# Seven block products in place of eight for half of a SwiGLU input matrix, on one TensorE

## The reference

```python
x = x + 0.5 * swiglu_ffn(rmsnorm(x, ffn1_norm), ffn1_w_in, ffn1_w_out)
proj = rmsnorm(x, mix_norm) @ w_in           # q, k, v of 16 heads, and 8 forget columns
... two kinds of attention, 8 heads each ...
x = x + mixed @ w_out
x = x + 0.5 * swiglu_ffn(rmsnorm(x, ffn2_norm), ffn2_w_in, ffn2_w_out)

def swiglu_ffn(x, w_in, w_out):
    gate, up = jnp.split(x @ w_in, 2, axis=-1)      # w_in is 2048 x 11008
    return (jax.nn.silu(gate) * up) @ w_out          # w_out is 5504 x 2048
```

## Time and profile before

| | |
|---|---|
| median of 3 runs | 1899.95 us (1899.06 to 1902.18) |
| profiled execution | 1897.12 us, its span 1895.3 us |
| mean granted clock of TensorE | 0.995 |
| instructions | 20376 |
| moved by DMA | 347.13 MB, mean 183 GB/s |

### The profile page before, as it was taken

The page is one execution under the profiler, slowest core; times in us unless marked ns, Lnnn a source line. Parts: engine busy times, 40 slices in busy tenths (PEclk is TensorE's granted clock), DMA queues, the critical chain, the costliest instruction groups (busy, mean ns, idle before and its releaser), DMA issues.

```text
span 1895.3 us, 20376 instructions
## 1 busy us (share of the span) xinstructions
PE 1858.9 (98%) x8470; PEld 1545.2 (82%) x8470; DVE 946.6 (50%) x1051; ACT 818.2 (43%) x971; POOL 26.9 (1%) x37
## 2 busy tenths in 40 slices
PE   6999999999999999999999999999999999999999
PEld 5888888888988888877777788888888888988887
DVE  4444444454544554365555555545444444444443
ACT  5444444444434444344444445444444444433332
POOL 1000000000000000000000000000000000000000
PEclk9999999999999999899999999999999999999999
DMA  6655555555655557344454455555655555556553
GB/s 225 213 197 181 197 185 192 190 187 172 206 194 186 181 200 241 108 137 156 145 166 155 164 170 177 180 198 179 198 180 199 182 195 180 192 185 210 202 202 116
DMA packets 175643, 347.13 MB, mean 183 GB/s; under 512 B 5808, under 2 KB 14064, under 8 KB 175424
## 3 DMA queue, kind: packets, MB, share of 16 engines
q1 hardware_dynamic: 172304, 337.92, 54.1%
q10 hardware_dynamic: 2080, 3.94, 0.6%
q0 software_dynamic: 1168, 3.97, 0.5%
HBM read 343.70 MB, written 3.68 MB: 183 GB/s over the span
## 4 chain that ended last, share of the span: by engine, by line
PE 93%; DVE 3%; ACT 2%; issue 1%; DMA 1%; ACTq 0%; DVEq 0%
PE acc L248 30%; PE acc L250 30%; PE acc L249 29%; ACT whi L458 2%; DVE wlo L676 1%; PE aux L275 1%; DMA x<-x 1%; PE aux L265 1%; PE aux L327 0%; DVE act_f L782 0%; PE aux L378 0%; PE aux L370 0%; PE aux L369 0%; PE aux L340 0%; PE aux L339 0%
## 5 line engine op out<-in xcount | busy, mean ns | idle before, releaser
L676 DVE TENSOR_TENSOR wlo<-raw,whi 128x1024 fp32r<-128x1024 f32 (+1 forms) x656 | 790.8, 1206 | 913.5 <-ACT whi L458 911.7
L458 ACT ACTIVATE whi<-raw 128x1024 fp32r<-128x1024 f32 (+1 forms) x656 | 684.6, 1044 | 1036.6 <-PE acc L250 1036.6
L248 PE MATMUL acc<-whi,xs 128*128 128x512 f32 (+1 forms) x1792 | 700.1, 391 | 3.7 <-DVE wlo L676 3.6
L250 PE MATMUL acc<-whi,xs 128*128 128x512 f32 (+1 forms) x1792 | 692.3, 386 | 0.0
L249 PE MATMUL acc<-wlo,xs 128*128 128x512 f32 (+1 forms) x1792 | 691.8, 386 | 0.0
L248 PEld LDWEIGHTS acc<-whi,xs 128*128 128x128 f32 x1792 | 337.4, 188 | 68.4 <-issue 5.1
L250 PEld LDWEIGHTS acc<-whi,xs 128*128 128x128 f32 x1792 | 337.3, 188 | 66.3
L249 PEld LDWEIGHTS acc<-wlo,xs 128*128 128x128 f32 x1792 | 337.6, 188 | 63.7
L248 PE MATMUL acc<-whi,act 128*128 128x512 f32 x688 | 268.1, 390 | 0.0
L250 PE MATMUL acc<-whi,act 128*128 128x512 f32 x688 | 267.7, 389 | 0.0
L249 PE MATMUL acc<-wlo,act 128*128 128x512 f32 x688 | 267.7, 389 | 0.0
(11 more groups left out here) (116 smaller groups left out, 519.4 us busy)
## 6 DMA issues: line engine op xcount, KB each, us to landing
raw<-ffn_w_in SPq DMA_DIRECT2D x160, 1024.0 KB, 4.9
raw<-ffn_w_out SPq DMA_DIRECT2D x80, 1024.0 KB, 4.9
raw<-w_in SPq DMA_DIRECT2D x48, 1024.0 KB, 5.0
raw<-w_out SPq DMA_DIRECT2D x16, 1024.0 KB, 4.9
raw<-ffn_w_in SPq DMA_DIRECT2D x16, 768.0 KB, 4.3
raw<-ffn_w_out SPq DMA_DIRECT2D x8, 768.0 KB, 4.3
x<-x ACTq DMA_DIRECT2D x4, 512.0 KB, 13.4
bias_vectors<-bias_vector POOLq DMA_DIRECT2D x1, 1536.0 KB, 9.0
```

The source lines that it names most:

```text
L248: mm(banks[b][:, 0:w], stationary[:, k, 0, tok], hi, start=k == 0, stop=False, skip_group_check=True)
L250: last = mm(banks[b][:, 0:w], stationary[:, k, 1, tok], hi, start=False, stop=k == k_total - 1, skip_group_check=True)
L458: A(whi[:, h % SLOTS, 0:n_el], raw[:, slot, first:first + n_el], ACT.Copy).then_inc(weights_hi, 1)
L676: V.tensor_tensor(wlo[:, h % SLOTS, 0:n_el], raw[:, slot, first:first + n_el], whi[:, h % SLOTS, 0:n_el].bitcast(f32), ALU.subtract).then_ ...
```

## The change

The first unit of each FFN is computed as before (`plain_unit`), with x_turn of part n placed right ahead of the halves that use it in the first FFN. In the other ten, k-tiles 0 to 7 are still plain halves (G0, G1 for the gate, U0, U1 for up: 8 halves of 12 matmuls). K-tiles 8 to 15 are taken as a 2 x 2 by 2 x 2 block product: blocks of tokens by k-tiles 8 to 11 and 12 to 15, and these by gate and up columns. Seven products (T1, B11, T2, B21, T3, B22, T4), each of two halves of 6 matmuls (`form`), take the place of eight. Their x side is a block of `xs` or one of four sums in `sf`, made once per FFN (`form_inputs`, `form_sums`, `form_splits`). Their weight side is a loaded piece, or one of four sums of pieces made on DVE in each unit (`sum_t1` to `sum_t4`, 128 x 2048 each), which are split like pieces. Parts of the results are copied out of PSUM by ACT (three copies a unit) and added by DVE (`w_done`, `gate_added` twice, `c11_done`).

`raw` has 6 slots in the FFNs. A slot is free when its last reader is done, which for B11 and B21 is `sum_t4`. SP issues the 8 pieces of a unit in the order of `LOAD`, and x's four parts stand in SP's queue too, each ahead of a weight piece.

The activation is kept in float32 (`act`), and `ffn_out` makes two passes over its 43 tiles with 1024 columns each, a half being one k-tile by 1024 columns; ACT and DVE split `act` once in each pass, two tiles at a time, into windows of 4 slots (`act_window_hi`, `act_window_lo`). Updates of x come after a pass: parts 0 and 1 in the second pass, parts 2 and 3 after it.

```diff
-RAW_SLOTS, SLOTS = 3, 4
+RAW_SLOTS, QKV_RAW_SLOTS, SLOTS, ACT_SLOTS = 6, 3, 4, 4
+ACT_PAIRS = -(-FT // 2)
...
+T1, B11, G0, T2, B21, T3, G1, B22, T4, U0 = 0, 2, 4, 6, 8, 10, 12, 14, 16, 18
+UNIT_HALVES = 22
+LOAD = {"B11": 0, "B12": 1, "B22": 2, "G0": 3, "B21": 4, "G1": 5, "U0": 6, "U1": 7}
...
+            def free(n):
+                for u in range(2):
+                    if IN_P[u] <= n < OUT_P[u]:
+                        j, i = (n - IN_P[u]) // 8, (n - IN_P[u]) % 8
+                        if j == 0:
+                            return weights_lo, IN[u] + 2 * i + 2
+                        if i in (LOAD["B11"], LOAD["B21"]):
+                            return sums_done, 4 * ((UNITS - 1) * u + j)
+                        last = {LOAD["B12"]: T3, LOAD["B22"]: B22, LOAD["G0"]: G0, LOAD["G1"]: G1, LOAD["U0"]: U0, LOAD["U1"]: U0 + 2}[i]
+                        return weights_lo, unit_half(u, j) + last + 2
+                    end = (QKV_P, END_P)[u]
+                    if OUT_P[u] <= n < end:
+                        c, q = (n - OUT_P[u]) // ACT_PAIRS, (n - OUT_P[u]) % ACT_PAIRS
+                        return weights_lo, OUT[u] + FT * c + min(2 * q + 2, FT)
+                return weights_lo, QKV + 2 * (n - QKV_P) + 2
...
+                    if j == 0:
                         for q in range(4):
-                            piece(n, w_in[:, 4 * q:4 * q + 4, col:col + UNIT_W[j]], 4, UNIT_W[j])
-                            n += 1
-                for c in range(N_OUT):
-                    for t in range(0, FT, 4):
...
+                            if u == 0:
+                                sp.dma_start(x[:, :, q * W:(q + 1) * W], x_rows[:, :, q * W:(q + 1) * W]).then_inc(x_loaded[q], 16)
+                            elif q == 3:
+                                sp.wait_ge(logit_ready, N_HEADS)
+                            piece(n + q, w_in[:, 4 * q:4 * q + 4, gate], 4, w)
+                        for q in range(4):
+                            piece(n + 4 + q, w_in[:, 4 * q:4 * q + 4, up], 4, w)
+                    else:
+                        piece(n + LOAD["B11"], w_in[:, 8:12, up], 4, w)
+                        piece(n + LOAD["B12"], w_in[:, 8:12, gate], 4, w)
+                        piece(n + LOAD["B22"], w_in[:, 12:16, gate], 4, w)
+                        piece(n + LOAD["G0"], w_in[:, 0:4, gate], 4, w)
+                        piece(n + LOAD["B21"], w_in[:, 12:16, up], 4, w)
+                        piece(n + LOAD["G1"], w_in[:, 4:8, gate], 4, w)
+                        piece(n + LOAD["U0"], w_in[:, 0:4, up], 4, w)
+                        piece(n + LOAD["U1"], w_in[:, 4:8, up], 4, w)
...
+            def form(h, bank_out, stationary, w, start):
+                for i in range(2):
+                    pe.wait_ge(weights_lo, h + i + 1)
+                    slot = (h + i) % SLOTS
+                    for k in range(2):
+                        hi, lo = whi[:, slot, k * w:(k + 1) * w], wlo[:, slot, k * w:(k + 1) * w]
+                        st_hi, st_lo = stationary(2 * i + k, 0), stationary(2 * i + k, 1)
+                        mm(bank_out[:, 0:w], st_hi, hi, start=start and i == 0 and k == 0, stop=False, skip_group_check=True)
+                        mm(bank_out[:, 0:w], st_hi, lo, start=False, stop=False, skip_group_check=True)
+                        last = mm(bank_out[:, 0:w], st_lo, hi, start=False, stop=i == 1 and k == 1, skip_group_check=True)
+                    last.then_inc(weights_used, 1)
...
+            def plain_unit(u):
+                Y, V, Z, X = unit_banks(0)
+                base, w, s = IN[u], UNIT_W[0], 2 * u
+                for hh in range(IN_HALVES):
+                    if u == 0 and hh % 2 == 0:
+                        x_turn(0, hh // 2)
+                    pe.wait_ge(x_ready, 16 * s + 2 * hh + 2)
+                    plain(base + hh, 2 * hh, (Z, X), (True, True), w, KT - 1)
+                    if u == 0 and hh == 7:
+                        small_products()
+                    if u == 1 and hh == 2:
+                        x_turn(2, 3)
+                for hh in range(IN_HALVES):
+                    plain(base + IN_HALVES + hh, 2 * hh, (V, Y), (True, True), w, KT - 1)
+            def unit(u, j):
+                Y, V, Z, X = unit_banks(j)
+                base, w, first = unit_half(u, j), UNIT_W[j], (UNITS - 1) * u + j - 1
+                blk0, blk1 = slice(0, P), slice(P, 2 * P)
+                if j == 1:
+                    pe.wait_ge(silu_done, 2 * (UNITS * u + 1))
+                    pe.wait_ge(s_ready, 4 * (u + 1))
+                    if u == 0:
+                        pe.wait_ge(vec_ready, 1)
+                else:
+                    pe.wait_ge(gate_added, 2 * first)
+                form(base + T1, Z, lambda k, t: sf[:, 0, k, t, :], w, True)
+                form(base + B11, Y, lambda k, t: xs[:, 8 + k, t, blk0], w, True)
+                pe.wait_ge(copied, 3 * first + 1)
+                for i in range(2):
+                    plain(base + G0 + i, 2 * i, (Z, X), (False, True), w, -1)
+                pe.wait_ge(copied, 3 * first + 2)
+                form(base + T2, Y, lambda k, t: sf[:, 1, k, t, :], w, False)
+                act_turn(u, j - 1)
+                form(base + B21, V, lambda k, t: xs[:, 12 + k, t, blk0], w, True)
+                pe.wait_ge(copied, 3 * first + 3)
+                form(base + T3, Y, lambda k, t: sf[:, 2, k, t, :], w, False)
+                for i in range(2):
+                    plain(base + G1 + i, 4 + 2 * i, (Z, X), (False, False), w, 7)
+                form(base + B22, Z, lambda k, t: sf[:, 3, k, t, :], w, False)
+                pe.wait_ge(w_done, first + 1)
+                form(base + T4, Y, lambda k, t: xs[:, 12 + k, t, blk1], w, False)
+                for i in range(4):
+                    plain(base + U0 + i, 2 * i, (V, Y), (False, False), w, 7)
 
...
+                first, w2 = (UNITS - 1) * u + j - 1, 2 * w
+                act_e.wait_ge(sums_done, 4 * first + 1)
+                for i in range(2):
+                    split(base + T1 + i, tsum[:, i * w2:(i + 1) * w2], w2)
+                loaded(n + LOAD["B11"])
+                for i in range(2):
+                    split(base + B11 + i, piece_half(n + LOAD["B11"], i, w2), w2)
+                loaded(n + LOAD["G0"])
+                split(base + G0, piece_half(n + LOAD["G0"], 0, w2), w2)
+                act_e.wait_ge(weights_used, base + T1 + 2)
+                A(gset[:, s, 1, 0:w], Z[:, 0:w], ACT.Copy).then_inc(copied, 1)
+                split(base + G0 + 1, piece_half(n + LOAD["G0"], 1, w2), w2)
+                act_e.wait_ge(sums_done, 4 * first + 3)
+                split(base + T2, piece_half(n + LOAD["B11"], 0, w2), w2)
+                act_e.wait_ge(weights_used, base + B11 + 2)
+                act_e.wait_ge(act_f_done, 2 * (UNITS * u + j))
+                A(p1s[:, 0:w], Y[:, 0:w], ACT.Copy).then_inc(copied, 1)
+                split(base + T2 + 1, piece_half(n + LOAD["B11"], 1, w2), w2)
+                loaded(n + LOAD["B21"])
+                for i in range(2):
+                    split(base + B21 + i, piece_half(n + LOAD["B21"], i, w2), w2)
+                split(base + T3, piece_half(n + LOAD["B12"], 0, w2), w2)
+                act_e.wait_ge(weights_used, base + T2 + 2)
+                A(gset[:, s, 0, 0:w], Y[:, 0:w], ACT.Copy).then_inc(copied, 1)
+                split(base + T3 + 1, piece_half(n + LOAD["B12"], 1, w2), w2)
+                act_copy(u, j - 1)
+                loaded(n + LOAD["G1"])
+                for i in range(2):
...
+                dve.wait_ge(weights_used, unit_half(u, j + 1) if j + 1 < UNITS else OUT[u])
                 dve.wait_ge(rstd_ready, 2 * u + 1)
-                if U:
-                    dve.wait_ge(act_psum, U)
-                for b in range(TB):
-                    dve.wait_ge(silu_done, 2 * U + b + 1)
-                    V.scalar_tensor_tensor(act_f[:, b, 0:w], acc[1][b][:, 0:w], rstd[:, 2 * u, b:b + 1], gate[:, b, 0:w],
-                                           ALU.mult, ALU.mult).then_inc(act_f_done, 1)
-
-            def act_split_lo(u, j):
-                tiles = UNIT_W[j] // P
-                for i in range(0, tiles, 2):
-                    n = min(2, tiles - i)
-                    dve.wait_ge(act_hi, OUT_HALVES * u + 2 * j + i // 2 + 1)
-                    V.tensor_tensor(act[:, 4 * j + i:4 * j + i + n, 1, :], aux[i // 2][:, 0:n * SEQ].rearrange("p (k s) -> p k s", k=n),
-                                    act[:, 4 * j + i:4 * j + i + n, 0, :].bitcast(f32), ALU.subtract).then_inc(act_ready, 1)
+                dve.wait_ge(silu_done, 2 * U + 2)
+                V.scalar_tensor_tensor(gset[:, s, 1, 0:w], Y[:, 0:w], rstd[:, 2 * u, 1:2], gset[:, s, 1, 0:w],
+                                       ALU.mult, ALU.mult).then_inc(act_f_done, 1)
+                if j:
+                    V.tensor_tensor(p1s[:, 0:w], V_[:, 0:w], p1s[:, 0:w], ALU.add).then_inc(c11_done, 1)
```

(83 more changed lines are left out.)

587 lines of the change are left out of this document (348 added, 239 removed).

## The result

Four runs of the changed kernel have a median of 1917.15 us (1915.90 to 1918.52), four of the kernel before on the same chip 1900.99 us. The ratio is 1.0087, with a 95% interval of 1.0071 to 1.0103: 0.9% slower. The profiled run is the slowest of the four (1918.52 us, span 1916.7 us, mean granted clock 0.987), and that of before, at 1897.12, lies under all the runs shown for it, so the spans differ by 21.4 us where the medians differ by 16.2.

The account below looks back on a forecast made before the run. The prediction took matmul issue on PE as the bound. It summed -0.2 (FFN units), +4.8 (start), +1.4 (qkv) and +1.2 (end) to +7.2 us on the profiled 1897.1, forecasting a median of 1907 us, range 1870 to 1926.

Parts of the forecast that it names:

- the likeliest case: Whole kernel: the saved matmul time is lost to stalls, 1907 us, own range 1898 to 1917; chance 0.42.
- What it removes: FFN units from the second on: 180 wide matmuls in place of 192, worth 53.1 us if PE stays the bound.
- What it adds on DVE: FFN units: more splits, four weight sums and PSUM additions make 37.6 us of DVE against PE's 41.7.
- The order followed: FFN units: PE stalls 1.70 us at G0 and 0.23 at G1, plus 0.09 each; unit 43.8 us without DMA.
- DMA: FFN units: at 347 GB/s pieces land late, sum_t1 starts 1.06 us late, G0 0.79 later; unit 44.58 us.
- rival B: FFN units: pieces land in time with DVE's chain as forecast, 12.6 us less, 1894 us; chance 0.22.
- Start: First unit: earlier x, but three stretches with 4.1 us of PE idle; +3.8 and 1 for the clock, +4.8 us.
- Pass boundary: ffn_out: splitting act twice costs DVE 0.30 us a half, put under edges at little or nothing, 0 in the sum.
- qkv and the end: qkv: x_update behind the fourth split, +1.4 us; end: four x_update operations in place of two, +1.2 us.
- The weighed rule: VectorE: next operation waits until the pipeline empties, every hold 0.09 us longer, sum 1931 us; judged contradicted by the four splits.
- Rival E: PE's clock falls after each pause, 2 us lost in 20 units, 1947 us; chance 0.06.
- Rival C: FFN units: PE remains the bound because the order overlaps better, 1854 us, up to 1885; chance 0.15.

Follow-up runs that it names:

- e4: Changed kernel with sum_t2, sum_t3 and sum_t4 each computing only 8 of their 2048 columns: 1872.19 us, ratio 0.9847 to the kernel before.
- e3: Changed kernel with sum_t2 alone computing only 8 of its 2048 columns: 1874.45 us, ratio 0.9867 to the kernel before.
- e5: Changed kernel with VectorE's unit order changed: swiglu after G0's splits, sum_t2 between them, sum_t4 ahead of B21's splits: 1895.76 us.
- e1: Changed kernel with the second ffn_out pass's first activation windows waiting for their own slots, not the whole first pass: 1905.97 us.
- e12: Changed kernel with swiglu after G0's splits, sum_t4 halved behind T2's splits, plus three repairs (second-pass window waits, x order at start, earlier x_update): 1851.45 us.
- e2: Changed kernel with x's first two parts turned and split ahead of the weights at the start, as in the kernel before: 1897.19 us.

## Why the prediction was right

The forecast of 1907 us lies 10 us under the median, which is at the upper end of the likeliest case's own range, 1898 to 1917. Its mechanism, a loss of the whole matmul gain to stalls of the splits, is what happened. That the number came as near is partly luck, since misses of opposite sign cancel. Point by point:

- **What it removes.** The pitch of 0.2267 and the product's time of 41.69 us a unit hold: e4 has 41.71.
- **What it adds on DVE.** A sum of 2048 lasts 2.29 and holds 2.21, as forecast (307.96 to 310.17). DVE is busy 86% of the FFN, against 90% expected.
- **The order followed.** The forecast put the stall at G0 at 1.70 us and 0.09 for the matmul behind it. The idle time in the rows is 1.55 in FFN 2; counted from where the next matmul was due, as the forecast counts, it is 1.71, and the slow first matmul adds 0.08. In FFN 1 the rows have 1.55 to 1.97, under the 2 to 2.5 that the profile was to show. The second stall, at G1, was put at 0.23 + 0.09 and is 0.06 + 0.11 (1353.61 to 1354.24). A unit without late pieces takes 43.73, forecast 43.8. e3 shows that the stall comes from sum_t2, and e5 that it needs no fewer instructions to go, only another order.
- **DMA.** In FFN 1 sum_t1 starts 0.4 to 1.0 us late in six of nine units, 4.9 in all; 1.06 in each was forecast. Units of 44.60 against 44.58 look exact and are not: two of them, of 45.4 and 45.6, are long because of the clock as well (0.79 granted from 132 to 140 and from 220 to 228, 7 and 8 matmuls 0.43 apart), behind pauses of 1.97. In FFN 2 the pieces are in time, so rival B holds there, and that is the -6.4. The next B11 is issued 10.4 us after T2 is used, as forecast. It is the landing that was priced too long: the rate of 347 GB/s, read from the first transfers, was too low, a full queue reaches 408 to 410, and B12 lands at 18.3 in FFN 2 (1303.78 to 1322.11) and at 19.0 in FFN 1 (275.42 to 294.42), forecast 19.3.
- **Start: mis-sized term.** Forecast +4.8, measured +12.2. The three turns and pauses of 4 us came as described, 4.99 us each from turn to matmul for the 5.0 forecast. The first turn waited for x until 5.38 (its terms, 0.74 + 1.85 + 1.5, make 4.1, not 4.2), so the first matmul started 1.0 us later than forecast (11.39 for 10.4). Most of the rest is the clock: behind the first pause and the three others 12, 13, 5 and 7 matmuls come 0.43 us apart, the distance of the 1.2 GHz level (0.50 granted from 24 to 28; from 12 to 16 the clock reads 1.00 although the matmuls are that far apart). The eight halves take 30.8 us in place of 21.8. For these 9.1 us the forecast had 2.4 in the first two halves and 1 beyond. The kernel before had shown one pause of 3.6 us with no slow stretch behind it; one row was a poor witness for four pauses.
- **Pass boundary: the step that failed.** "Splitting act twice in ffn_out costs DVE 0.30 a half", under the edges at little or nothing, looked at the price of the instructions and not at what they wait for. The wait for a whole pass of ffn_out was in the diff and has no term in the sum. It cost 5.5 and 3.9 us in the profile, 11.2 in medians, and e1 takes it away.
- **qkv and the end.** +4.0 for 1.4. The halves ahead of the forget products take 2.4 us more (27.8 for 25.4), with a pause of 0.95 before the moved turn and the turn itself. The forget products take 1.8 more (17.6 for 15.9), since more of them run at the lower clock. +1.5 for 1.2: four updates of x, 2.48 us from 1911.00.

So the size is nearer than its parts: +16.8 us of misses at the start and the two boundaries, +2.6 in qkv, +0.8 in FFN 1 and +0.3 at the end, less 6.3 in FFN 2, 14.2 in the profile and 10 in the medians. The weighed rule of the Trainium skill, "VectorE: DVE Perf Modes", The DRAIN you can't avoid, gave 1931; the trace does not agree, four splits last 4.62 us and sum and split start 2.21 apart, and the units have the length that the shorter hold gives. The same paragraph of the Trainium skill goes on that an operation that is not held starts earlier, and that is what these rows show, so the 1931 rested on half of it. The other rule of the Trainium skill, "TensorE: Matmul & The Clock Gate", What's actually happening (throttled by default, released by activity), agrees with the start and with 636 to 640 (0.50 granted from 24 to 28 and there); behind the pause of 3.60 at 1793.74 the trace does not show it. Rival E was priced at every pause; it came behind all four pauses of the start, one boundary and two units. Rival C said 1854 if the order overlapped better; as given it does not, but e12 with another order and the three repairs is at 1851. Open are why FFN 1's pieces land later than FFN 2's, and why some pauses of the same length lower the clock and others do not.

## What to carry to other kernels

Fewer matmuls help only as far as the engine that prepares their operands keeps its lead at every single split: follow the order of that engine instruction by instruction, and break a long operation or move it away from where two splits follow closely. Before moving it, ask what its end releases; an operation that frees the slot at the head of a transfer queue must stay early. And for each edit read not only what it costs but what it waits for: one semaphore value and an order of turns cost 31 us here, more than half of the whole gain that was sought.

## What the runs showed that I had not expected

- Several 1024 KB pieces in flight move at 408 to 410 GB/s (292 to 294 and others), where the first transfers of the kernel show 347.
- TensorE fell to 1.2 GHz behind pauses of 3.96 us at the start and behind one of 3.60 at 636.23, and not behind an equal one at 1793.74, though in e2 behind both. Behind most of the 20 pauses of 1.5 to 2.0 us it stayed at full clock; behind two of 1.97 it fell, behind a third of 1.97 (355.67) it did not.
- A pause costs about 0.3 us more than the idle time in the rows even when the granted clock reads 1.00 (units of 42.39 with a pause of 0.38, against 41.71 with none). About 0.16 is the way of counting and 0.11 the first matmul behind the pause, and a loss of 0.17 us at G1 shows no idle time at all.
